# A one-core transformer layer with grouped experts: the order of three code variants inside the job loop, and a sorting pass cut in two

## The reference, cut to what matters

```python
def grouped_moe(x, w_router, router_bias, w_gate, w_up, w_down):
    scores = sigmoid(x @ w_router)                    # 256 tokens, 16 experts
    ... # the best group of 4 experts, then the best 2 experts inside it, gates normalised
    for e in range(N_EXPERTS):
        h = silu(x @ w_gate[e]) * (x @ w_up[e])       # 2048 -> 1024
        y = y + combine[..., e:e + 1] * (h @ w_down[e])   # 1024 -> 2048
    return y
```

## Time and profile before

| | |
|---|---|
| median of 3 runs | 1568.07 us (1567.37 to 1568.51) |
| the profiled execution, its own time | 1566.21 us |
| its span, first to last instruction | 1564.4 us |
| TensorE matmul busy | 1302.0 us, 83% |
| DMA, mean rate | 358 GB/s |
| jobs in this input | 16: job 0, and 15 in the loop |

### The profile page before, as it was taken

One profiled execution on the slowest core, in us unless ns is written; L12 is line 12 of the kernel. 1 busy time (PEld: TensorE's weight loads), 2 busy tenths in 40 slices (PEclk: granted clock), 3 DMA queues, 4 the chain that ended last, 5 costly groups with the idle time before them and its releaser, 6 DMA issues.

```text
span 1564.4 us, 19544 instructions
## 1 busy us (share of the span) xinstructions
PE 1302.0 (83%) x7868; PEld 538.8 (34%) x7869; DVE 428.6 (27%) x797; ACT 143.8 (9%) x252; POOL 76.2 (5%) x138
## 2 busy tenths in 40 slices
PE   3899999899989888789589679967867867877876
PEld 2556444455445553222133132221321321221221
DVE  3122785767565410101010111111111111111112
ACT  3000001332100122000000000000000000000000
POOL 0121000121221000000000000000000000000000
PEclk9999999999999889889789988989988988988987
DMA  9999558665898366999699989969999999999997
GB/s 382 420 409 412 237 222 329 228 240 218 310 360 323 148 244 260 420 421 421 276 422 420 373 331 420 420 278 422 422 422 421 422 421 421 422 422 421 422 422 304
DMA packets 84376, 559.77 MB, mean 358 GB/s; under 512 B 9680, under 2 KB 9680, under 8 KB 22608
## 3 DMA queue, kind: packets, MB, share of 16 engines
q1 hardware_dynamic: 69408, 502.49, 78.2%
q0 software_dynamic: 14320, 52.01, 9.0%
q10 hardware_dynamic: 576, 4.19, 0.7%
HBM read 556.57 MB, written 2.10 MB: 357 GB/s over the span
## 4 chain that ended last, share of the span: by engine, by line
PE 45%; DMA 42%; issue 5%; DVE 5%; ACT 2%; SPq 0%; DVEq 0%; POOL 0%; ACTq 0%; POOLq 0%
DMA ring<-w_up_dram 15%; DMA ring<-w_gate_dram 14%; PE ps L828 7%; PE ps L568 7%; PE ps L833 7%; DMA rope_heads<-w_down_dram 6%; PE ps L856 3%; DMA ring<-w_half_dram 3%; PE ps L671 3%; DMA ring<-w_in_dram 3%; PE ps L562 2%; PE ps L850 2%; PE ps L789 2%; PE ps L801 2%; PE ps L573 2%
## 5 line engine op out<-in xcount | busy, mean ns | idle before, releaser
L828 PE MATMUL ps<-ring,early 128*32 128x256 f32 x2304 | 179.8, 452 | 113.0 <-issue 58.4
L833 PE MATMUL ps<-ring,early 128*64 128x512 f32 x672 | 167.1, 619 | 27.6 <-DMA ring<-w_gate_dram 19.0
L1467 DVE TENSOR_TENSOR big<-ps,big 128x1024 f32<-128x1024 f32 x64 | 75.4, 1220 | 364.3 <-PE ps L789 364.3
L828 PEld LDWEIGHTS ps<-ring,early 128*32 128x32 f32 x2304 | 73.6, 124 | 232.0 <-issue 116.9
L568 PE MATMUL ps<-ring,big 128*128 128x512 f32 x320 | 146.1, 598 | 0.0
L1124 DVE SCALAR_TENSOR_TENSOR halves<-ring,silu_c,halves 128x1024 f32<-128x1024 f32 x96 | 123.2, 1283 | 40.4 <-DMA ring<-w_half_dram 34.8
L671 PE MATMUL ps<-ring,big 128*128 128x512 f32 x256 | 113.8, 601 | 1.3 <-ACT big L1015 1.3
L833 PEld LDWEIGHTS ps<-ring,early 128*64 128x64 f32 x672 | 41.7, 139 | 137.7 <-issue 65.9
L568 PEld LDWEIGHTS ps<-ring,big 128*128 128x128 f32 x320 | 59.1, 191 | 69.5 <-issue 69.4
L671 PEld LDWEIGHTS ps<-ring,big 128*128 128x128 f32 x256 | 48.6, 193 | 59.4 <-issue 59.4
L856 PE MATMUL ps<-ring,bufA 128*64 128x512 f32 x224 | 58.4, 666 | 8.7 <-DVE early L1485 8.7
(11 more groups left out here) (316 smaller groups left out, 1062.8 us busy)
## 6 DMA issues: line engine op xcount, KB each, us to landing
ring<-w_gate_dram SPq DMA_DIRECT2D x128, 1024.0 KB, 23.8
ring<-w_up_dram SPq DMA_DIRECT2D x64, 1024.0 KB, 25.9
ring<-w_down_dram SPq DMA_DIRECT2D x64, 1024.0 KB, 27.2
ring<-w_half_dram POOLq DMA_DIRECT2D x96, 512.0 KB, 6.7
ring<-w_mix_dram SPq DMA_DIRECT2D x32, 1024.0 KB, 11.3
big<-w_up_dram SPq DMA_DIRECT2D x32, 1024.0 KB, 24.4
big<-w_down_dram SPq DMA_DIRECT2D x32, 1024.0 KB, 25.5
ring<-w_in_dram SPq DMA_DIRECT2D x28, 1024.0 KB, 9.3
```

The lines of the kernel that those rows point to most:

```text
L828: mm = pe.matmul(out_b[0][BASE * f:BASE * (f + 1), :], rows[0][:, k, :], w[:, kk, f * 256:(f + 1) * 256], start=(k == 0), stop=(k == KT - 1))
L833: mm = pe.matmul(out_b[1][REST * f:REST * (f + 1), :], rows[1][:, k, :], w[:, kk, f * N:(f + 1) * N], start=(k == 0), stop=(k == KT - 1))
L1467: tt(y, banks[:, 2 * h:2 * h + 2, :].rearrange("p a n -> p (a n)"), y, ALU.add).then_inc(done, 1)
```

## The change

Three edits.

- In `any_job` on TensorE, ScalarE and VectorE the branches are turned round. The table's flags now say "few" (at most 32 rows) and "some" (at most 64); in the layout few comes first, then some, then full, then the end of the loop. The same holds for the copy of job 0. One more column of `vcol` on VectorE makes the new flag.
- `sort_rows` takes the blocks that it sorts. In job 0 the first eight blocks are sorted behind the up chunks, before the wait for `hidden_ready`; the other eight between the fourth and the fifth chunk of `w_down`. ScalarE saves the first eight behind its Silu and the others behind the copy of `hT`, and only then copies the rows of job 1.
- `oh_all` moves from `work` to `probs`; so VectorE waits until the matmuls that read `oh_first` are done (`gathered`) before it writes it.

```diff
-        vcol = sb("vcol", [CAND, 13])
+        vcol = sb("vcol", [CAND, 14])
-        oh_all = work[:].rearrange("p (t s) -> p t s", t=TT)
+        oh_all = probs[:]
...
-            def sort_rows():
+            def sort_rows(blocks):
                 pe.wait_ge(oh_ready, 1)
-                for k in range(KT):
+                for k in blocks:
...
                 for m, out_b in ((0, Gb), (1, Ub)):
-                    if m == 1 and first:
-                        sort_rows()
-                    elif m == 1:
+                    if m == 1 and not first:
                         scatter(j, 0)
...
-                if not first:
+                if first:
+                    sort_rows(range(0, KT // 2))
+                else:
                     scatter(j, 1)
                 pe.wait_ge(hidden_ready, j + 1)
...
                 for i in range(8):
+                    if i == 4 and first:
+                        sort_rows(range(KT // 2, KT))
                     w = arrived(16 + i)
...
-                with pe.If(wide):
-                    with pe.If(full):
+                with pe.If(few):
+                    experts(j, (0,), first)
+                with pe.Else():
+                    with pe.If(some):
+                        experts(j, (1,), first)
+                    with pe.Else():
                         experts(j, (0, 1), first)
-                    with pe.Else():
-                        experts(j, (1,), first)
-                with pe.Else():
-                    experts(j, (0,), first)
...
+            def save_sorted(blocks):
+                for k in blocks:
                     act.wait_ge(sort_done, k + 1)
                     act.activation(xg_all[:, k, :], S[k % 2], ACT.Identity, bias=modcol[:, 3, k, 0:1],
                                    scale=scale_ffn[:, k:k + 1]).then_inc(sorted_saved, 1)
...
                 last.then_inc(silu_saved, 1)
+                if first:
+                    save_sorted(range(0, KT // 2))
                 act.wait_ge(ehT_done, j + 1)
...
                 last.then_inc(ehT_saved, 1)
+                if first:
+                    save_sorted(range(KT // 2, KT))
+                    act.wait_ge(sorted_saved, KT)
                 job_rows(at)
...
-            ts(vcol[:, 12:13], vcol[:, 8:9], k_("blk_lo")[0:CAND, :], float(REST), ALU.subtract, ALU.is_gt)
+            ts(vcol[:, 12:13], vcol[:, 8:9], k_("blk_lo")[0:CAND, :], float(REST), ALU.subtract, ALU.is_le)
+            ts(vcol[:, 13:14], vcol[:, 8:9], k_("blk_lo")[0:CAND, :], float(BASE), ALU.subtract, ALU.is_le)
...
             dve.wait_ge(table_ready, 1)
+            dve.wait_ge(gathered, KT)
```

More of the change, by code:

```diff
@@ L743, in _ @@
                                   start=True, stop=True)
-                        pe.matmul(Z[0][0:1, 256 + JOBS:256 + 2 * JOBS], vcol[:, 1:2], onehot_j[:],
+                        pe.matmul(Z[0][0:1, 256 + JOBS:256 + 2 * JOBS], vcol[:, 13:14], onehot_j[:],
                                   start=True, stop=True)
@@ L864, in any_job @@
             def any_job(j, first):
-                wide = pe.value_load(n_i[0:1, JOBS:JOBS + 1] if first else n_i[0:1, bass.ds(j + JOBS, 1)],
+                few = pe.value_load(n_i[0:1, JOBS:JOBS + 1] if first else n_i[0:1, bass.ds(j + JOBS, 1)],
                                      min_val=0, max_val=1)
-                full = pe.value_load(n_i[0:1, 3 * JOBS:3 * JOBS + 1] if first else n_i[0:1, bass.ds(j + 3 * JOBS, 1)],
+                some = pe.value_load(n_i[0:1, 3 * JOBS:3 * JOBS + 1] if first else n_i[0:1, bass.ds(j + 3 * JOBS, 1)],
                                      min_val=0, max_val=1)
-                with pe.If(wide):
-                    with pe.If(full):
+                with pe.If(few):
[4 more added lines that the diff above has]
+                    with pe.Else():
                         experts(j, (0, 1), first)
-                    with pe.Else():
-                        experts(j, (1,), first)
-                with pe.Else():
-                    experts(j, (0,), first)
             any_job(0, True)
@@ L1046, in job_rows @@
                 return copy(xg, span[:, :, 0:BLK]).then_inc(xg_ready, 1)
-            def job_evac(j, parts, at, first):
-                for k in range(KT if first else 0):
+            def save_sorted(blocks):
+                for k in blocks:
                     act.wait_ge(sort_done, k + 1)
@@ L1052, in job_evac @@
                                    scale=scale_ffn[:, k:k + 1]).then_inc(sorted_saved, 1)
+            def job_evac(j, parts, at, first):
                 act.wait_ge(slot_free, j * JCH + used_job(7))
@@ L1060, in job_evac @@
                 last.then_inc(ehT_saved, 1)
+                if first:
+                    save_sorted(range(KT // 2, KT))
+                    act.wait_ge(sorted_saved, KT)
                 job_rows(at)
             def any_job(j, first):
-                wide = act.value_load(n_i[0:1, JOBS:JOBS + 1] if first else n_i[0:1, bass.ds(j + JOBS, 1)],
+                few = act.value_load(n_i[0:1, JOBS:JOBS + 1] if first else n_i[0:1, bass.ds(j + JOBS, 1)],
                                       min_val=0, max_val=1)
-                full = act.value_load(n_i[0:1, 3 * JOBS:3 * JOBS + 1] if first else n_i[0:1, bass.ds(j + 3 * JOBS, 1)],
+                some = act.value_load(n_i[0:1, 3 * JOBS:3 * JOBS + 1] if first else n_i[0:1, bass.ds(j + 3 * JOBS, 1)],
                                       min_val=0, max_val=1)
@@ L1070, in any_job @@
                                     min_val=0, max_val=2 * SEQ - 1)
-                with act.If(wide):
-                    with act.If(full):
+                with act.If(few):
+                    job_evac(j, (0,), at, first)
+                with act.Else():
+                    with act.If(some):
+                        job_evac(j, (1,), at, first)
+                    with act.Else():
                         job_evac(j, (0, 1), at, first)
[L1074 to L1077, removed]
             any_job(0, True)
-            act.wait_ge(sorted_saved, KT)
             with act.Fori(1, jobs) as j:
@@ L1500, in any_job @@
             def any_job(j, first):
-                wide = dve.value_load(n_i[0:1, JOBS:JOBS + 1] if first else n_i[0:1, bass.ds(j + JOBS, 1)],
+                few = dve.value_load(n_i[0:1, JOBS:JOBS + 1] if first else n_i[0:1, bass.ds(j + JOBS, 1)],
                                       min_val=0, max_val=1)
-                full = dve.value_load(n_i[0:1, 3 * JOBS:3 * JOBS + 1] if first else n_i[0:1, bass.ds(j + 3 * JOBS, 1)],
+                some = dve.value_load(n_i[0:1, 3 * JOBS:3 * JOBS + 1] if first else n_i[0:1, bass.ds(j + 3 * JOBS, 1)],
                                       min_val=0, max_val=1)
-                with dve.If(wide):
-                    with dve.If(full):
+                with dve.If(few):
+                    hidden_product(j, (0,), first)
+                with dve.Else():
+                    with dve.If(some):
+                        hidden_product(j, (1,), first)
+                    with dve.Else():
                         hidden_product(j, (0, 1), first)
[L1508 to L1511, removed]
             any_job(0, True)
```

## The result

| | before | after |
|---|---|---|
| median | 1568.10 us (1567.37 to 1573.48, 6 runs) | 1556.28 us (1553.58 to 1562.32, 6 runs) |
| ratio | | 0.9922, 95% interval 0.9899 to 0.9945 |
| the profiled execution, its own time | 1566.21 us | 1553.58 us |
| its span | 1564.4 us | 1551.8 us |

A forecast was written before the change was run, and what follows sets the result against it. TensorE's code fetches bound the pairs of full and few, the weight DMA the rest. Savings of 10.4 by job 2 and 20 in jobs 2 to 7 sum to 30.4 us: 1538 us, own range 1520 to 1552, wider 1513 to 1558.

The forecast's parts named there:

- The terms of the sum: Whole kernel: job 2 starts 10.4 us earlier, jobs 2 to 7 save 20, jobs 8 to 15 save 0.
- a demand: TensorE waiting for a 16 KB block of its code, about 250 instructions; taken as 6.0 to 6.4 us at turns.
- Entry to job 0: Ahead of job 0: idle time shrinks from 6.0 to about 1.5 us, 4.5 us less; start at 557.3.
- The sort: Job 0: up no longer waits for the sort matmuls, the DMA never runs dry; job 1's matmuls end at 653.4, not 675.4.
- Job 1 to 2, two demands, 12.5 us: First turn to full: loop end and full both waited for, 12.5 us in place of 1.0; job 2 starts at 666.0.
- Full to few 5.5, few to full 6.4: Turns in jobs 2 to 7: one block waited for at each, 5.5 us in place of 15.8 and 6.4 in place of 1.0.
- Jobs 8 to 15: Pairs of few and some: five blocks called anew per pair, all ahead of time and hidden by the DMA; 0 us.
- slower: Rival, chance 0.04: few and some thrash over nine blocks in jobs 8 to 15; seven waits a pair give 1582 us.
- Stalls moved: Rival, chance 0.13: two waits at each turn between full and few, 12.5 and about 9 us; 1558, up to 1564.
- Nearly no demands: Rival, chance 0.12: code fetches hardly stall TensorE, so the DMA never idles; 62.7 us less, 1506, up to 1520.
- no change: Rival, chance 0.03: the first job alone gains and the turns give it all back; 1568 us.
- the ring: Later estimate of how TensorE holds its code blocks, fitted to 59 packets before and 96 after; it forecasts packet counts and stops.

The follow-up runs named there:

- With 44: The changed kernel with 44 never-run TensorE instructions ahead of the loop; 1537.23 us.
- Experiments 1 and 2: Against the kernel before: only the sort in two halves with the `oh_all` move, 1552.04 us; only the new order of variants and flags, 1569.19 us.
- The kernel with 124: The changed kernel with 124 never-run TensorE instructions ahead of the loop; 1545.13 us.
- Experiment 3: The changed kernel with its loop code moved by 44 never-run TensorE instructions; 1537.23 us, ratio 0.9799.
- the kernel before with 40: The kernel before the change with 40 never-run TensorE instructions ahead of the loop; 1553.88 us.
- 76 and 60: The changed kernel with 76 or 60 never-run TensorE instructions ahead of the loop; 1548.54 us and 1547.69 us.
- all three padded kernels: Never-run instructions added: 40 or 80 to the kernel before, 1553.88 and 1547.23 us; 80 to the old order with the sort in two halves, 1538.40 us.

## Why the prediction went wrong

- *The terms of the sum*: which blocks are held, and so which are demanded at which turn, is my assumption, and no run shows it; nor does one show the price of a demand, 6.0 to 6.4 us, or that the 15.8 us were three of them. What the traces show in its place are the packets in each stop: one from few to full, where I had one demand; three from job 1 to 2, where I had two; none in the first stop behind a full job and one in the second, where I had one demand; three behind the jobs with some, where I had none; five behind the full jobs of the kernel before, where I had three. Stops with one packet at the turns took 4.7 to 7.8 us.
- *Entry to job 0*: a gap of 1.5 us foretold, 1.6 measured. Right. That these are register loads no run shows; the trace has 1.60 us of issue, with no packet in it. That the start came within 1 us too (557.3 foretold, 558.3 measured) is partly luck: in the kernels with this entry it lay anywhere from 555.7 to 565.1.
- *The sort*: right in place and mechanism. Chunk 12 was foretold to be issued at 559.3; SyncE's timeline of the changed kernel has

```profile
559.42 2.92 SPq L408 DMA_DIRECT2D ring<-w_up_dram  x4
```

  Job 1's last matmuls end at 656.5 in place of 653.4: 1.0 from the start, and the stream moved 408 GB/s from 560 to 655 us where 421 had been taken. Job 1's second stop is the likely cause: it frees slots late, and from 620 to 630 us the stream has only 339 GB/s. With 44, without that stop, it moves 420 there. Experiments 1 and 2 show that the split carries the gain.
- *Job 1 to 2, two demands, 12.5 us*: 12.7, with three packets. Right. Job 2 starts at 669.2, 3.2 us late in all.
- *Full to few 5.5, few to full 6.4*: 5.8 and 6.8. Near in size, but the first by luck. The 5.8 come in two pieces. The first piece is only 2.9, near the 3 that the prediction named as its lower value: the packet ahead of it moves between 747 and 749 us, before full job 2 ends at 749.1. The other 3.0, with one packet (753.44 to 754.40), are the block's edge, which was not in the sum. With 44, where the second stop is gone and the gaps are 2.8, 2.8 and 2.7 us, jobs 2 to 7 take 377.7 us, just as the prediction had it, mostly because two errors cancel: 2.7 us too much for the gap, and 2.4 too little for a few job, which then waits for its weights (38.8 us for 36.4). In the changed kernel, with the edge, and with job 3's down chunks waiting for the DMA (1.41 us in the row at 791.70), the first pair takes 131.2 us (669.22 to 800.45) in place of 127.7. Jobs 2 to 7 took 384.1 us, 20 less had meant 378.9: 5.2 us short.
- *Jobs 8 to 15: "five are called anew in each pair, but all ahead of time ... the DMA hides it. 0."* This is the step that failed. Nine packets move in the pair from 1053.3 to 1174.0 us, not five; three of them go with the stop of 11.7 us and a fourth with the 2.6 us at the edge. Behind the step stands an assumption on which block goes when another comes, which had been fitted to 59 packets and which no run shows. The kernel with 124 speaks against it: 79 packets with the least recently used block thrown out, 95 measured. The other half is the edge: no term of the sum asked where in a block a job begins. From job 8's start to the end of the span the changed kernel takes 498.5 us, the one before 489.1: 9.4 us. The first three pairs have 5.0 of them (1.3, 1.9, 1.9), the last pair and the end 4.4, of which 1.8 lie in the last scatter (2.09 and 2.81 us, 1.14 and 1.99 before).

The shortfall of 17.8 us against the profiled execution's forecast is these terms: 3.2 + 5.2 + 9.4. Experiment 3 confirms the last: with the stops of jobs 8 to 15 gone, the same stretch takes 489.1 us (1531.6 less 1042.5).

The rival *slower* named what happened, stops in jobs 8 to 15, and got near its price: nothing as long as they fit in the slack of 27 us that TensorE has in a pair there, where the first three pairs paid 1.3 to 1.9 us each. *Stalls moved* came close in time (1558) for another reason: the turns of jobs 2 to 7 did shrink, from 16.8 us of idle in a pair (15.8 + 1.0) to 12.6 (5.8 + 6.8). *Nearly no demands* and *no change* are out, by the 12.7 us of the turn 1 to 2 and by the interval.

The forecast took the layout's blocks as given by the variants' lengths. What neither it nor any rival had is that moving the loop's code counts for more than the order: 19 us between two kernels that run the same instructions. With 44 the median of 1537 is the forecast's 1538; that is no proof of its count of blocks, which had no place in it for the 44. Two of its side sums are off by half a microsecond (668.5 adds up to 668.9, 1506 to 1505), which changes nothing.

## What to carry to other kernels

Where a timeline has "issue" gaps at a loop's turns, count the instruction queue's packets stretch by stretch; before judging an edit that moves code, run both versions with a few dozen dead instructions ahead of the loop, for otherwise a change of 20 us can be nothing but placement (80 dead instructions took 21 us off the kernel before). A fit to one kernel's counts leaves open what the engine holds: look for two estimates that fit and forecast by both. Gaps of an engine cost what the stream behind it cannot make up, here some 8 us of 60 (14.2 to 15.9 in each of four pairs) in jobs 8 to 15, and nearly all in jobs 2 to 7, where TensorE is the bound: with 44, the gaps at their six turns are 24.5 us less than before (24.1 for 48.6), and the jobs 21.2 us shorter.

## What the runs showed of the hardware

- From job 0 on, each stop of TensorE with "issue" of more than 2.2 us ended 1.2 to 1.9 or 3.2 to 3.8 us behind the end of a packet of queue 8, in all twelve kernels.
- In the kernel before, the turns without packets left gaps of at most 1.1 us, which end with VectorE or a DMA. At the turns, stops with one packet in them lasted 4.7 to 7.8 us (one of 6.4, in the kernel before with 40, had two), with three (some begun up to 0.5 us ahead of the stop) 10.7 to 13.7, with five 14.6 to 16.1. Behind the full jobs in the new order they lasted 2.5 to 3.1 with no packet in them; the last one had ended 3.2 to 3.4 us before TensorE went on.
- At the edge taken for a block's, the matmul behind it started 5.3 to 5.7 us after the job's first in full jobs (with 76 and 60) and 3.5 to 4.0 in few jobs of the changed kernel; TensorE stood 1.5 to 3.5 us there, with one packet each time.
- Three pairs of jobs 8 to 15, of 592 matmuls and 592 weight loads each, ran with 2 packets in all with 44, and with nine a pair in the changed kernel. In every kernel of the new order the packets are as many as the ring gives, in the old order it misses all three padded kernels (76, 68 and 79 measured); so the runs leave open how many blocks are held and which goes.
- Behind a stop TensorE was slow for some matmuls more: after the 6.9 us ahead of job 4 with 44, the first L834 chunk took 3.67 us in place of 1.94, at a granted clock of 0.52 (0.50 in the gap, where TensorE did nearly nothing).
- The same work ahead of job 0 ended up to 9 us apart between profiled executions (555.7 to 564.6 us); no run here says why.
